# Conditioning weights in chunks of one contraction row over two sections, 512 columns to a column tile

## The reference, cut to what matters

```
mod  = silu(c)     @ w_mod[l] + b_mod[l]        # w_mod[l]: 1024 x 6144
modc = silu(c_ctx) @ w_mod[l] + b_mod[l]
sh_a, sc_a, gt_a, sh_f, sc_f, gt_f = split(mod, 6)          # sections 0 to 5; the same of modc
h  = rmsnorm(x, g_attn) * (1 + sc_a) + sh_a
x  = x + gt_a * mixers(h)                       # conv, neighbourhood attention, windowed attention
h2 = rmsnorm(x, g_ffn) * (1 + sc_f) + sh_f
x  = x + gt_f * moe(h2)                         # 32 experts, top 2
```

## Time and profile before

| | |
|---|---|
| time, median of 3 runs | 1396.62 us (1391.85 to 1399.54) |
| span of the profiled execution | 1396.2 us, mean granted clock 0.953 (its time outside the span is not listed) |
| PE busy | 1211.0 us, 87% of the span |
| DVE busy | 648.9 us, 46% |
| ACT busy | 437.4 us, 31% |
| DMA | 356.13 MB, mean 255 GB/s |
| conditioning matmuls (L909) | 768 records (two for one instruction), 48 loads of 1024 KB |
| chain that ended last | PE 78%, DVE 9%, issue 5%, DMA 5%, ACT 3% |

### The profile page before, as it was taken

How to read it: one execution, slowest core, us unless ns; L and a number is a source line. 1 busy time by engine, 2 the same in 40 slices (tenths; PEclk the granted TensorE clock), 3 DMA queues, 4 the chain that set the end, 5 groups by cost and what they waited for, 6 DMA issues and landing times.

```text
span 1396.2 us, 21881 instructions
## 1 busy us (share of the span) xinstructions
PE 1211.0 (87%) x8870; PEld 927.1 (66%) x8870; DVE 648.9 (46%) x1462; ACT 437.4 (31%) x1026; POOL 138.4 (10%) x175
## 2 busy tenths in 40 slices
PE   4999887999998988899999559988998878889982
PEld 2788754788887856566666359965998755556550
DVE  1545686455446383322221185667776544332313
ACT  2533367433333440000000264356665500000001
POOL 1510000111003320100000101001011200000001
PEclk9899999999999989999999869999999989999996
DMA  9952145333315497999999875248555849999995
GB/s 348 320 158 91 61 168 166 121 97 114 92 61 208 167 343 281 370 408 414 396 388 408 322 251 151 91 150 259 181 182 210 306 198 419 422 422 419 421 422 196
DMA packets 130230, 356.13 MB, mean 255 GB/s; under 512 B 20600, under 2 KB 82288, under 8 KB 106448
## 3 DMA queue, kind: packets, MB, share of 16 engines
q1 hardware_dynamic: 117568, 317.68, 61.3%
q0 software_dynamic: 6528, 18.59, 4.1%
q10 hardware_dynamic: 6032, 18.43, 3.4%
HBM read 332.62 MB, written 22.06 MB: 254 GB/s over the span
## 4 chain that ended last, share of the span: by engine, by line
PE 78%; DVE 9%; issue 5%; DMA 5%; ACT 3%; POOL 0%; SPq 0%; DVEq 0%; POOLq 0%; ACTq 0%
PE banks L969 33%; PE banks L1198 16%; PE banks L1212 8%; PE banks L1190 5%; PE banks L1137 4%; PE banks L909 2%; PE banks L1065 2%; DMA ring<-in_w_mod 2%; PE banks L1080 2%; PE banks L1050 2%; DMA ring<-in_w_e_down 1%; DMA ring<-in_w_e_up 1%; PE banks L1162 1%; DMA att<-expert_rows,slots_u 1%; DVE arena L2225 1%
## 5 line engine op out<-in xcount | busy, mean ns | idle before, releaser
L1901 DVE TENSOR_TENSOR w_lo_r<-ring,w_hi_r 128x256 fp32r<-128x256 f32 x480 | 222.7, 474 | 246.2 <-ACT w_hi_r L1511 244.9
L1511 ACT ACTIVATE w_hi_r<-ring 128x256 fp32r<-128x256 f32 x480 | 197.4, 416 | 303.0 <-PE banks L969 253.9
L1198 PE MATMUL banks<-ring,arena 128*64 128x256 f32 x2032 | 235.9, 386 | 41.1 <-issue 24.5
L1198 PEld LDWEIGHTS banks<-ring,arena 128*64 128x64 f32 x2032 | 165.0, 139 | 102.3 <-issue 51.3
L969 PE MATMUL banks<-h_hi_r,w_hi_r 128*128 128x512 f32 (+1 forms) x640 | 221.9, 347 | 5.8 <-DVE h_lo_r L1831 4.5
L969 PE MATMUL banks<-h_lo_r,w_hi_r 128*128 128x512 f32 (+1 forms) x640 | 220.3, 344 | 0.0
L969 PE MATMUL banks<-h_hi_r,w_lo_r 128*128 128x512 f32 (+1 forms) x640 | 220.0, 344 | 0.0
L969 PEld LDWEIGHTS banks<-h_hi_r,w_hi_r 128*128 128x128 f32 x640 | 122.7, 192 | 22.8 <-issue 4.1
L1212 PE MATMUL banks<-ring,att 128*64 128x512 f32 x456 | 120.0, 613 | 16.0 <-issue 13.6
L969 PEld LDWEIGHTS banks<-h_lo_r,w_hi_r 128*128 128x128 f32 x640 | 122.8, 192 | 13.9
L969 PEld LDWEIGHTS banks<-h_hi_r,w_lo_r 128*128 128x128 f32 x640 | 122.6, 192 | 14.0
(11 more groups left out here) (246 smaller groups left out, 1606.6 us busy)
## 6 DMA issues: line engine op xcount, KB each, us to landing
ring<-in_w_e_gate SPq DMA_DIRECT2D x64, 1024.0 KB, 9.5
ring<-in_w_e_up SPq DMA_DIRECT2D x63, 1024.0 KB, 9.6
ring<-in_w_e_down SPq DMA_DIRECT2D x57, 1024.0 KB, 10.5
ring<-in_w_mod SPq DMA_DIRECT2D x48, 1024.0 KB, 6.0
ring<-in_w_in SPq DMA_DIRECT2D x38, 1024.0 KB, 5.4
expert_rows<-arena ACTq DMA_DIRECT2D x30, 512.0 KB, 8.8
ring<-in_w_o SPq DMA_DIRECT2D x8, 1024.0 KB, 5.3
ring<-in_w_branch SPq DMA_DIRECT2D x8, 640.0 KB, 4.5
```

Of the source, the lines that this page charges most:

```text
L1198: ins = mm(banks[e * CAP:(e + 1) * CAP, bank, 0:DE], x[:, k, e * CAP:(e + 1) * CAP], w[:, k * DE:(k + 1) * DE], start=k == 0, stop=k == KD ...
L1511: fn(w_hi[:, u % AHEAD, :, :], chunk(key)[:, q * KU:(q + 1) * KU, :], ACT.Copy).then_inc(w_hi_ready, 1)
L1901: v.tensor_tensor(w_lo[:, u % AHEAD, :, :], chunk(key)[:, q * KU:(q + 1) * KU, :], w_hi[:, u % AHEAD, :, :].bitcast(F32), ALU.subtract).th ...
```

## The change

- A unit now is half of the contraction of a *pair* of sections: a chunk is one contraction row by 2048 columns (`MW`), and four of them make a unit. Units 2p and 2p + 1 together make sections 2p and 2p + 1. The names `(l, u)` in `MOD_IN`, `MOD_ROUTE` and `MODS` are units.
- In `mod`, each of four column tiles works on 512 columns: four matmuls a chunk, not eight. Rows of the even section lie in partitions 0 and 32 (and one above), those of the odd section in 64 and 96.
- `mod_add` is 128 x 512, and the second unit of a pair adds to what the first left. The FFN scale is formed after unit 5, on 64 partitions; `g_rows` holds one layer, and POOL reloads it for layer 1.
- A section is complete with its pair's second unit (`mod_whole`). The turns take 64 weight columns in two column tiles: 16 instructions a section, not 32. At the start both sections are turned after the eighth chunk.
- Placement: four units (sixteen chunks) in each attention, two in layer 0's routing, none in layer 1's routing.

```diff
+MW = 2 * D
+MOD_IN = [[(0, 2), (0, 3), (0, 4), (0, 5)], [(1, 2), (1, 3), (1, 4), (1, 5)]]
+MOD_ROUTE = [[(1, 0), (1, 1)], []]
+MODS = [(0, 0), (0, 1)] + MOD_IN[0] + MOD_ROUTE[0] + MOD_IN[1] + MOD_ROUTE[1]
...
+        def mod_whole(l, sec):
+
+            return MOD_AT[(l, sec // 2 * 2 + 1)] + 1
...
-                    sec, j2 = divmod(c, 4)
-                    src = t["w_mod"][l].rearrange("(p k) n -> p k n", k=KD)[:, 2 * j2:2 * j2 + 2, sec * D:(sec + 1) * D]
+                    pr, k = divmod(c, KD)
+                    src = t["w_mod"][l].rearrange("(p k) n -> p k n", k=KD)[:, k, pr * MW:(pr + 1) * MW]
...
+                else:
+                    pool.wait_ge(mod_out, mod_whole(0, 4))
+                for s in range(2):
+                    pool.dma_start(g_rows[s:64:32, :], t["g_ffn"][l].rearrange("(j n) -> j n", j=2)).then_inc(g_rows_in, 16)
...
-                for k in (0, 1):
-                    for q in range(4):
-                        ins = mm(banks[32 * q:32 * q + 32, mod_bank(l, sec), 0:CW], cond32[:, 2 * j2 + k, :],
-                                 w[:, k, q * CW:(q + 1) * CW], start=j2 == 0 and k == 0, stop=j2 == 3 and k == 1)
+                for q in range(4):
+                    ins = mm(banks[32 * q:32 * q + 32, mod_bank(l, u), :], cond32[:, 4 * (u % 2) + j, :],
+                             w[:, q * 512:(q + 1) * 512], start=j == 0, stop=j == 3)
...
+            def turn_rows(l, sec, bank, at):
+
+                rows, p0 = mod_rows_of(l, sec)
+                for k in range(KD):
+                    for j in range(2):
+                        ins = mm(banks[64 * j:64 * j + 64, bank, at + 2 * k:at + 2 * k + 2], rows[:, k::KD],
+                                 ident[:, p0 + 32 * j:p0 + 32 * j + 2], start=True, stop=True)
+                return ins
...
-                    columns(0, 1)
-                    pe.wait_ge(col_ready, 1)
-                    for j2 in range(4):
-                        mod(0, 0, j2)
+                    for j in range(4):
+                        mod(0, 1, j)
+                    columns(0, 1)
                     columns(0, 0)
...
+                dst = modr[:, l, u // 2, :]
+                if u % 2:
+                    dve.wait_ge(mod_out, n)
+                ins = v.tensor_tensor(dst, banks[:, mod_bank(l, u), :], dst, ALU.add)
+                if u == 5:
+
                     link(ins)
-                    dve.wait_ge(g_rows_in, 16 * 2 * DEPTH)
-                    ins = v.scalar_tensor_tensor(dst, dst, 1.0, g_rows[:, l, :], ALU.add, ALU.mult)
+                    dve.wait_ge(g_rows_in, 32 * (l + 1))
+                    ins = v.scalar_tensor_tensor(dst[0:64], dst[0:64], 1.0, g_rows[:, :], ALU.add, ALU.mult)
```

More of the change, by code:

```diff
@@ L129, in weight_stream @@
         if l == 0:
-            out += [("mod", 0, 4 * sec + j) for _, sec in MODS[:2] for j in range(4)]
+            out += [("mod", 0, 4 * u + j) for _, u in MODS[:2] for j in range(4)]
         out += [("in", l, c) for c in IN_ORDER]
-        out += [("mod", k, 4 * sec + j) for k, sec in MOD_IN[l] for j in range(4)]
+        out += [("mod", k, 4 * u + j) for k, u in MOD_IN[l] for j in range(4)]
         for n in range(4):
@@ L135, in weight_stream @@
         out += [("wo", l, c) for c in range(4)]
-        out += [("mod", k, 4 * sec + j) for k, sec in MOD_ROUTE[l] for j in range(4)]
+        out += [("mod", k, 4 * u + j) for k, u in MOD_ROUTE[l] for j in range(4)]
         out += [(kind, l, e) for kind in ("eg", "eu") for e in (0, 1)]
@@ L528, in mod_chunk, with mod_rows_of @@
         def mod_chunk(key):
-            return ring[:, AT[key] % SLOTS, :].rearrange("p (k n) -> p k n", n=D)
+            return ring[:, AT[key] % SLOTS, 0:MW]
+        def mod_rows_of(l, sec, s=None):
+            p0 = 64 * (sec % 2)
+            if s is None:
+                return modr[:, l, sec // 2, :], p0
+            return modr[p0 + s:p0 + 64:32, l, sec // 2, :], p0
         def landed(eng, key, i=None):
@@ L888, in _ @@
                 if l == 0:
+                    ffn_scale_rows(1)
                     load_rev(pool, 1)
@@ L929, in ffn_columns @@
                 for sec, bank in ((4, 6), (3, 7)):
[L930 to L944 removed]
+                    pe.wait_ge(mod_out, mod_whole(l, sec))
+                    turn_rows(l, sec, bank, 0).then_inc(f_cols_done, 1)
+            def columns(l, sec):
+                pe.wait_ge(mod_out, mod_whole(l, sec))
+                turn_rows(l, sec, *COL_BANK[(l, sec)]).then_inc(cols_done, 1)
             def turn_xn(l, tt, ks):
@@ L1364, in _ @@
                     pe.wait_ge(ident_in, 16)
-                    for j2 in range(4):
-                        mod(0, 1, j2)
-                        if j2 in (1, 2):
-                            for tt in (2 * j2 - 2, 2 * j2 - 1):
+                    for j in range(4):
+                        mod(0, 0, j)
+                        if j in (1, 2):
+                            for tt in (2 * j - 2, 2 * j - 1):
                                 turn_xn(0, tt, range(KD if tt < 2 else KD - 2))
+                    for j in range(4):
+                        mod(0, 1, j)
                     columns(0, 1)
-                    pe.wait_ge(col_ready, 1)
-                    for j2 in range(4):
-                        mod(0, 0, j2)
                     columns(0, 0)
@@ L1389, in _ @@
                 pe.wait_ge(upd_ready, 4 * QT0[l] + 3 * QT[l])
-                for j2 in range(4):
-                    mod(*MOD_ROUTE[l][0], j2)
+                for k, u in MOD_ROUTE[l][:1]:
+                    for j in range(4):
+                        mod(k, u, j)
                 pe.wait_ge(upd_ready, 4 * (QT0[l] + QT[l]))
                 ffn_columns(l)
-                pe.wait_ge(mod_out, MOD_AT[MOD_ROUTE[l][0]] + 1)
+                for unit in MOD_ROUTE[l][:1]:
+                    pe.wait_ge(mod_out, MOD_AT[unit] + 1)
                 turn_h(l)
                 route(l)
-                for k, sec in MOD_ROUTE[l][1:2]:
-                    for j2 in range(4):
-                        mod(k, sec, j2)
+                for k, u in MOD_ROUTE[l][1:]:
+                    for j in range(4):
+                        mod(k, u, j)
                 ranks(l)
-                for k, sec in MOD_ROUTE[l][2:]:
-                    for j2 in range(4):
-                        mod(k, sec, j2)
                 experts(l)
@@ L1804, in columns @@
             def columns(l, sec):
-                turned = banks[:, COL_BANK[(l, sec)], 0:2 * KD].rearrange("p (k s) -> p k s", s=2)
+                bank, at = COL_BANK[(l, sec)]
+                turned = banks[:, bank, at:at + 2 * KD].rearrange("p (k s) -> p k s", s=2)
                 if sec:
                     dve.wait_ge(g_col_in, 16)
-                dve.wait_ge(cols_done, 2 * l + (1 if sec else 2))
+                dve.wait_ge(cols_done, 2 * l + (1 if sec and l else 2))
                 if l:
@@ L2378, in _ @@
                 residual(l)
-                mod_add(*MOD_ROUTE[l][0])
+                for unit in MOD_ROUTE[l][:1]:
+                    mod_add(*unit)
                 ffn_norm(l)
@@ L2386, in _ @@
                 place(l, False)
-                for k, sec in MOD_ROUTE[l][1:]:
-                    mod_add(k, sec)
+                for unit in MOD_ROUTE[l][1:]:
+                    mod_add(*unit)
                 if l == 0:
```

66 lines of the change are left out of this document (23 added, 43 removed).

## The result

The changed kernel takes 1417.14 us (median of 4 runs, 1412.53 to 1426.38) against 1398.08 (4 runs) of the kernel before on the same chip: a ratio of 1.0142 with a 95% interval of 1.0103 to 1.0180. It is slower, by 19 us where 4.2 were forecast, and lies above the range of 1391 to 1409. Run again beside the experiments it gave 1.0134 (1.0100 to 1.0168).

What follows compares the result with a forecast made beforehand. PE was taken to bound layer 1's attention, DVE and ACT to pace layer 0's latent steps, and DMA the experts. Terms 1.2 + 1.9 + 4.4 - 0.4 - 2.9 = +4.2 on 1396.6 gave 1400.8 us, range 1391 to 1409.

Steps and rivals of the forecast that it cites:

- Step 4: Layer 1's attention, 12 chunks to 16: four more at 1.00 each, adds +0.7, -0.3 from the chunk's form; +4.4 us.
- Step 1: The wide chunk itself: 1.00 us alone, bounds 0.85 to 1.05; -0.3 us over layer 1's attention's twelve old chunks.
- Step 7: The rest, such as the scale row's reload and rows_out DMAs: costs nothing on the path.
- Steps 2, 5 and 6: Start +1.2 us, its two turned sections 2 x 1.18; layer 0's routing -0.4; layer 1's routing 2.9 saved.
- Step 3: Layer 0's attention, 12 chunks to 16: chunks +0.1 and +0.5, adds +1.3; +1.9 us, bounds +0.3 to +4.
- C: Rival: attention's dependency chain amplifies chunk and add delays, 6.9 us in layer 0, 4.4 + 1 in layer 1; 1409.5, chance 0.15.
- B: Rival: chunks become cheap and the routing gain stands; 1393 us, or 1391 if unexplained gaps vanish too; chance 0.25.

Runs made afterwards that it cites:

- odd ends: Changed kernel, early adds, layer 1's sixteen chunks spread so that every unit ends on an odd step (3, 5, 9, 11): 1409.48 us, 1.0082.
- four-tile turns: Changed kernel with each turn again in four column tiles of 32 weight columns, 32 matmuls a section: 1409.92 us, 1.0089.
- tile-by-tile run: Changed kernel with late adds, four-column-tile turns and units ending on odd steps, its turn matmuls reordered, one column tile after another: 1414.18 us, 1.0101.
- late add: Changed kernel with DVE's add moved from ahead of the copy to behind the scaling in both attention loops: 1402.24 us, 1.0033.
- second profile: Changed kernel run again unaltered beside the first experiments, as their reference: 1417.35 us, 1.0134.
- kernel of three edits: Changed kernel with adds behind DVE's scaling, turns of 32 weight columns in four tiles, and layer 1's units ending on odd steps: 1392.51 us, 0.9959.

## Why the prediction was wrong, step by step

**Step 4, layer 1's attention, is the step that failed.** It said "two of the four now falling on even steps where PE is not about to attend: +0.7". The count and the place were right and the conclusion was the wrong way round. On an even step PE is about to *turn*: its next `turn_p` waits for DVE's scaling, DVE takes its work in order, and ahead of that scaling stood an add that waits for PE's second chunk. So PE waits for DVE, which waited for PE. I looked at the length of the add (0.69 us) and not at what the add itself waits for, nor at which PE instruction needs what is queued behind it. The four chunks cost about what the step said, 3.8 us (45.2 against 41.3 from first to last `attend`) or 3.2 (42.5 against 39.3), where it had 4.0. The even ends cost 7.0 us (68.5 against 61.5), in a step that had 0.7 for all adds together. Of these PE idles 4.7 us (12.3 against 7.6), above all in the two waits of 2.40 and 2.47, and is busy 2.2 us longer (56.1 against 54.0) with the same matmuls, some of them at a clock that fell to 0.50 behind the second wait (983.10 to 985.00).

**Step 1, the chunk itself:** a wide chunk takes 1.00 us on its own (945.09 to 946.09, odd ends), as an old one does, and four take 3.64 us where the same timeline has 3.66 for four old ones. Half the matmuls and weight loads saved nothing here, and the -0.3 of the sum has nothing behind it: with twelve chunks the two forms take 41.3 and 41.0 us with the early add, 39.3 both with the late one.

**Step 7, the rest:** it did not foresee the 3.2 us behind layer 1's attention. They come from the clock's fall at the end of that attention, seen in both profiles of the changed kernel. That the idle of 2.13 us brings it down is argued and not shown, since the profiles with four-tile turns and with odd ends have the same idle and a stage of 124.9 and 124.8 us.

**Steps 2, 5 and 6, the turns.** The upper bound of step 2 multiplied two factors, twice the columns and half the overlap, 4 x 1.18 = 4.7 us for two sections; I took the middle, 2 x 1.18 = 2.4. Measured is 4.01, near the bound. The tile-by-tile run shows the second factor by itself: with no neighbour in another tile a turn takes three times as long. How much of the 125 ns is the wider weight load and how much the missing tiles stays open, as no run has 64 weight columns without a neighbour. At the **start** the sum came out right by luck (col_add at 37.70 against 36.80, +0.9, forecast +1.2), as two errors cancel: the turns cost 1.6 us more than taken, and the last chunk ended at 31.59 + 1.06 = 32.65, not at 33.07 + 1.94 = 35.01, 2.4 us sooner where I had allowed 0.5. Of the 2.4, 0.9 is the clock: this chunk's matmuls ran at 1.00 here and at 0.50 before. The other 1.5 is the data. In the ten profiles with wide chunks the last one starts 17.1 to 17.5 us after the first, in the four with old chunks 18.8 to 19.2; that the longer runs of bytes do it is likely and was not tried by itself. In **layer 0's routing** (-0.4 forecast, +0.3 measured) the unexplained 1.47 us gap was gone, and the slower turns took its place. With four-tile turns and one section less that stretch took 36.9 us in one profile and 38.4 to 39.5 in three others, where the clock was 0.56 to 0.69 over the turns of h and not 1.00. In **layer 1's routing** f_add came 1130.55 - 1125.7 = 4.8 us behind the last projection matmul, against 1103.94 - 1097.5 = 6.4 before by the same measure: 1.6 us sooner, where 2.9 were forecast. The 1.9 us that the two-tile turns cost there more than cover the difference. The way to the first gate matmul took back another 1.1, by the clock: that stretch takes 9.9 us in the four profiles where its granted clock is 0.67, both of the changed kernel among them, and 8.6 to 9.1 in the ten where it is 0.78 to 0.83.

**Step 3, layer 0's attention:** +3.1 against +1.9, within the bounds (+0.3 to +4). Its sixteen chunks have only odd ends; the late add takes 4.1 us off, where the step had 2.3 for all adds. With the late add the stage takes 73.3 us from first to last `attend` with sixteen wide chunks (74.9 in one profile, with 3.4 us at the lower clock) and 73.4 with twelve old ones, so the four more chunks cost nothing there and the +3.1 was the adds.

**The rivals.** C had the mechanism in kind, a chain in which a chunk and a wide add hold up DVE's scaling, and forecast 1409.5. It put the price on layer 0's context steps and gave layer 1 one microsecond of it; it belongs to layer 1's even ends, where two chunks stand on one step. Its chance of 0.15 was too low: the very rows on which the forecast rested show a PE chain in which `turn_p` follows the chunk at once. B, cheap chunks, falls: its routing gain was eaten by the turns. The sum by steps, forecast against measured: +1.2 and +0.9, +1.9 and +3.1, +4.4 and +10.5, 0 and +3.2, -0.4 and +0.3, -2.9 and -1.2. That makes +16.8 of the 20.8 us by which the second profile's span is longer. The rest is in two stages that the first profile shows otherwise: 1.2 us in the start, and 3.1 in layer 0's branches, where the second profile has two stretches of 3.4 us at a granted clock of 0.50 and the first none.

The two rules of the Trainium skill that the prediction weighed gave 1.2 and 2.4 us for the start's two turned sections, and the trace has 4.01. "TensorEngine Tiling (Array Packing)", section Instruction Overhead, would make half as many matmuls half the price; here they were 1.9 times the price. By the columns of the weight load ("TensorE: Matmul & The Clock Gate", section LDWEIGHTS) alone nothing would be gained or lost by two tiles; that misses the overlap between tiles.

## What to carry to other kernels

Before putting an operation into an in-order engine's loop, ask what it waits for and which engine needs what is queued behind it: an add of 0.7 us held PE up for 2.4 us on an even step and for 0.35 at the cheapest odd one, and moving it behind the result that PE waits for was worth 15 us here. In the kernel before it was 2.7 us by the two attentions, too little for its runs to show. Spreading work evenly over steps is no neutral choice when steps come in pairs; let units end where their consumer has cover. Small matmuls such as these turns gain from neighbours in other column tiles: interleave the tiles, and do not merge two narrow tiles into a wide one to save instructions. Before a difference of 1 to 3 us between two profiles is put down to an edit, compare the granted clock of the stretch.

## What the runs showed of the hardware

- Small fp32 matmuls with two streamed columns: 33 ns each with 32 weight columns and four column tiles in turn, 101 ns each with the same matmuls tile by tile, 125 ns each with 64 weight columns and two tiles in turn. The two forms that were seen at different clocks did not follow it. The four-tile turn of two sections takes 2.18 us in the start at a granted clock of 0.50 and 2.12 us in layer 0's routing at 1.00; the two-tile turn takes 4.01 us at 0.52 and at 0.80. Windows over the turns, first the kernel of three edits, then the changed kernel:

```profile
33.10:35.20 2.10, 2.10 (x128) 2.07 (x128) 0.00 (x0) 1.00 (x4) 2.10 (x4) 0.50 1.13 355
477.70:479.70 2.00, 2.00 (x132) 2.00 (x124) 0.87 (x2) 0.00 (x0) 0.00 (x0) 1.00 1.05 416
```

```profile
33.50:37.40 3.90, 3.90 (x64) 3.89 (x64) 0.00 (x0) 1.34 (x4) 3.90 (x7) 0.52 1.09 379
485.30:489.20 3.90, 3.90 (x68) 3.90 (x64) 0.87 (x2) 0.00 (x0) 0.00 (x0) 0.80 1.01 404
```

- An fp32 add on DVE out of PSUM: 0.69 us for 128 x 512 (x12, all between 0.681 and 0.693), and a scaling on 64 partitions of the same width 0.68. At 128 x 256 the two operations take the same time (0.425), so half the partitions saved nothing.
- The same idle of PE may bring its clock down or not: 2.13 us with 0.50 behind it in two profiles and 1.00 in another; 1.85 us with 0.56 behind it and 1.86 with 1.00. A stage of one profile can differ by 3 us for this alone (128.1 against 124.9).
